# Attention: high and low halves of the turned weights side by side in one tile, one matmul of 512 columns for both

## The reference, cut to what matters

```
s = q[:, q0:q1] @ k[:, :q1].T                      # per head
s = s + cum[q0:q1, None] - cum[None, :q1]          # forget gate sums
p = softmax(where(causal, s, -inf))
o[q0:q1] = p @ v[:, :q1]
return (o * silu(gate)) @ w_out
```

## Time and profile before

| | us |
|---|---|
| median of 3 runs | 2338.66 (2337.63 to 2339.77) |
| the profiled execution | 2337.15 |
| its span | 2335.4 |
| PE busy in the span | 2318.9 (99%) |
| DVE, ACT, POOL busy | 1349.1 (58%), 1114.3 (48%), 621.9 (27%) |
| the attention, first V to last | about 748 to 1525 |

### The profile page before, as it was taken

The page is one execution under the profiler, slowest core; times in us unless marked ns, Lnnn a source line. Parts: engine busy times, 40 slices in busy tenths (PEclk is TensorE's granted clock), DMA queues, the critical chain, the costliest instruction groups (busy, mean ns, idle before and its releaser), DMA issues. The chain is left out here.

```text
span 2335.4 us, 36441 instructions
## 1 busy us (share of the span) xinstructions
PE 2318.9 (99%) x13373; PEld 2026.8 (87%) x13373; DVE 1349.1 (58%) x2772; ACT 1114.3 (48%) x2060; POOL 621.9 (27%) x718
## 2 busy tenths in 40 slices
PE   9999999999999999999999999999999999999998
PEld 7888889999887999999999999988888888888887
DVE  4221121232012999899998999956535565768733
ACT  2111111231113989889898898822024565657300
POOL 0000000010000455566556665536410000000344
PEclk9999999999999999999999999999999999999999
DMA  6444443242216365456654566286624354448672
GB/s 209 138 130 111 118 126 113 105 136 104 68 64 168 90 143 122 116 128 149 144 120 117 128 147 147 87 257 198 209 81 136 114 156 133 135 136 307 211 235 98
DMA packets 221306, 328.77 MB, mean 141 GB/s; under 512 B 17469, under 2 KB 144765, under 8 KB 215309
## 3 DMA queue, kind: packets, MB, share of 16 engines
q1 hardware_dynamic: 220616, 325.91, 48.7%
q0 software_dynamic: 512, 0.53, 0.1%
HBM read 199.89 MB, written 126.48 MB: 140 GB/s over the span
## 5 line engine op out<-in xcount | busy, mean ns | idle before, releaser
L1018 DVE TENSOR_TENSOR at_pl<-at_tps,at_ph 128x512 fp32r<-128x512 f32 (+3 forms) x640 | 372.0, 602 | 27.5 <-ACT at_ph L919 27.4
L919 ACT ACTIVATE at_ph<-at_tps 128x512 fp32r<-128x512 f32 (+3 forms) x640 | 317.3, 534 | 63.1 <-PE at_ops L849 41.7
L380 ACT ACTIVATE pa_stg<-pa_ps 128x512 fp32r<-128x512 f32 (+1 forms) x120 | 71.7, 598 | 575.4 <-PE pa_ps L272 569.5
L829 PE MATMUL at_tps<-ident,at_probs 128*128 128x128 f32 x2176 | 328.5, 273 | 1.3 <-ACT at_probs L909 1.3
L849 PE MATMUL at_ops<-at_ph,at_val 128*128 128x256 f32 (+1 forms) x1152 | 322.9, 298 | 1.4 <-DVE at_pl L1018 1.4
L909 ACT ACTIVATE at_probs<-at_probs,at_least 128x128 f32<-128x128 f32 (+15 forms) x256 | 308.4, 1205 | 17.5 <-DVE at_least L1007 17.5
L849 PE MATMUL at_ops<-at_pl,at_val 128*128 128x256 f32 (+1 forms) x1152 | 299.7, 281 | 0.0
L272 PE MATMUL pa_ps<-pa_xh,pa_wh 128*128 128x512 f32 x760 | 298.8, 393 | 0.0
L272 PE MATMUL pa_ps<-pa_xh,pa_wl 128*128 128x512 f32 x760 | 297.3, 391 | 0.0
L272 PE MATMUL pa_ps<-pa_xl,pa_wh 128*128 128x512 f32 x760 | 296.9, 391 | 0.0
L829 PEld LDWEIGHTS at_tps<-ident,at_probs 128*128 128x128 f32 x2176 | 256.1, 140 | 25.1 <-ACT at_probs L909 1.6
(11 more groups left out here) (203 smaller groups left out, 4553.1 us busy)
## 6 DMA issues: line engine op xcount, KB each, us to landing
at_q<-q_halves SPq DMA_DIRECT2D x45, 512.0 KB
at_k<-k_halves SPq DMA_DIRECT2D x45, 512.0 KB
q_halves<-pa_stg SPq DMA_DIRECT2D x32, 512.0 KB, 3.8
k_halves<-pa_stg SPq DMA_DIRECT2D x32, 512.0 KB, 3.7
v_halves<-pa_stg SPq DMA_DIRECT2D x32, 512.0 KB, 2.9
y_gated<-re_work SPq DMA_DIRECT2D x32, 512.0 KB, 2.9
at_val<-v_halves SPq DMA_DIRECT2D x15, 1024.0 KB, 13.3
pa_wst<-in_attn_w_in SPq DMA_DIRECT2D x14, 1024.0 KB, 7.1
```

Of the source, the lines that this page charges most:

```text
L380: nc.scalar.activation(out, source(kind, s), func, scale=scale).then_inc(evac_h, 1)
L829: mm = nc.tensor.transpose(tps[c % TB][:, k, :], probs[s % ROWS][:, t0:t0 + P], ident[:, :])
L919: nc.scalar.activation(ph[g % 2][:, j * PB:j * PB + n, i % 2 * P:(i % 2 + 1) * P], tps[c % TB][:, 0:n, :], ACT.Copy).then_inc(high_out, 1)
L1018: nc.vector.tensor_tensor(pl[g % 2][at], tps[c % TB][:, 0:n, :], raw(ph[g % 2][at]), ALU.subtract)\
```

## The change

- `ph` and `pl` become one tile `halves[b]` of 128 x 2 x 16 x 256, with the high half at index 0 and the low half at 1. H and L write the same shapes as before, into it.
- Each key tile has one matmul with the 2 x 256 columns of both halves, into the whole bank `ops[b]`: columns 0 to 255 are the sum over the high halves, 256 to 511 the sum over the low ones. In the last key tile it is 2 x 128 columns.
- M's first copy takes 64 x 2 x 256 instead of 64 x 256; its second part goes to one of two extra slots of `att`. M's second copy is as before, and takes the columns of the high half alone: the product of low values and low weights, which was in the sum before, is left out.
- POOL adds the two parts of `att` with one more addition, and waits for it before it adds `low_sum`.
- The transposed inverse sums of group n (n % 4 == 2) go to the other bank, `ops[1 - b]`, since `ops[b]` is full. So PE waits for the move of group n - 1 before the transpose, and before the first V of group n + 1, which writes `ops[1 - b]`, it waits for the copy of the inverse sums. The wait before the groups with n % 4 == 0 goes.
- The tiles in SBUF are put in another order; the unused space shrinks from 5 x 128 to 128 elements.

```diff
@@ weigh (PE)
-                    if g % HG == 0:
-                        wait(pe, rden_out, (it * GROUPS + g) // HG)
+                    if g % HG == HG - 1:
+                        wait(pe, rden_out, (it * GROUPS + g) // HG + 1)
                 for kt in range(lo, hi):
                     c0 = P if kt == KT - 1 else 0
-                    for t in (ph, pl):
-                        mm = nc.tensor.matmul(ops[b][:, 0, c0:GW], val[hp][:, kt, :], t[b][:, kt, c0:GW],
-                                              start=(kt == 0 and t is ph), stop=(kt == KT - 1 and t is pl))
+                    mm = nc.tensor.matmul(ops[b][:, :, c0:GW], val[hp][:, kt, :], halves[b][:, :, kt, c0:GW],
+                                          start=(kt == 0), stop=(kt == KT - 1))
                 if hi == KT:
                     mm.then_inc(weighed, 1)
                     if g % HG == HG - 2:
                         f = (it * GROUPS + g) // HG
                         wait(pe, rden_ready, f + 1)
-                        nc.tensor.transpose(ops[b][0:2 * HG, 1, 0:P], rden[:, f % 2, :], ident[:, :]).then_inc(rden_turned, 1)
+                        wait(pe, moved, 2 * (it * GROUPS + g))
+                        nc.tensor.transpose(ops[1 - b][0:2 * HG, 0, 0:P], rden[:, f % 2, :], ident[:, :]).then_inc(rden_turned, 1)
@@ move (ACT)
-                    nc.scalar.activation(rden_rows[:, f % 2, :], ops[b][0:2 * HG, 1, 0:P], ACT.Copy).then_inc(rden_out, 1)
+                    nc.scalar.activation(rden_rows[:, f % 2, :], ops[1 - b][0:2 * HG, 0, 0:P], ACT.Copy).then_inc(rden_out, 1)
                 wait(act, summed, n - 1)
                 wait(act, gated, 2 * (n - AR + 1))
-                nc.scalar.activation(att[:, n % AR, :], ops[b][0:HEAD_DIM, 0, :], ACT.Copy).then_inc(moved, 1)
+                slot, extra = n % AR, AR + n % 2
+                nc.scalar.activation(att[:, slot:extra + 1:extra - slot, :], ops[b][0:HEAD_DIM, :, :], ACT.Copy)\
+                    .then_inc(moved, 1)
@@ add_halves (POOL)
                 pool.wait_ge(moved, 2 * n + 2)
+                nc.gpsimd.tensor_tensor(att[:, n % AR, :], att[:, n % AR, :], att[:, AR + n % 2, :], ALU.add)\
+                    .then_inc(joined, 1)
+                pool.wait_ge(joined, n + 1)
                 nc.gpsimd.tensor_tensor(att[:, n % AR, :], att[:, n % AR, :], low_sum[:, n % 2, :], ALU.add)\
                     .then_inc(summed, 1)
```

More of the change, by code:

```diff
@@ L572, in attend @@
         a = Alloc(nc, ctx, stage)
-        q1, q2, k1, k2, val, probs, ph, pl = ({} for _ in range(8))
+        q1, q2, k1, k2, val, probs, halves = ({} for _ in range(7))
         def rows(t, name, k, dt=F32R):
@@ L579, in values, with turned_rows @@
             val[k] = a.sb(f"val{k}", [P, QT, P], F32R)
-        def turned_rows(t, name, k):
-            t[k] = a.sb(f"{name}{k}", [P, QT, GW], F32R)
+        def turned_rows(k):
+            halves[k] = a.sb(f"turned{k}", [P, 2, QT, GW], F32R)
         rows(q1, "q1_", 0)
@@ L589, in attend @@
         rows(k2, "k2_", 1)
-        turned_rows(ph, "ph", 0)
+        values(1)
+        rows(probs, "probs", 1, F32)
         rows(q1, "q1_", 1)
         rows(q2, "q2_", 1)
-        turned_rows(pl, "pl", 0)
-        values(1)
-        rows(probs, "probs", 1, F32)
+        turned_rows(0)
         rows(k2, "k2_", 0)
         values(0)
-        turned_rows(ph, "ph", 1)
-        turned_rows(pl, "pl", 1)
+        turned_rows(1)
         for k in range(2, ROWS):
@@ L604, in attend @@
         scale = a.sb("scale", [HEAD_DIM, 2, HG, GW])
-        att = a.sb("att", [HEAD_DIM, AR, GW])
+        att = a.sb("att", [HEAD_DIM, AR + 2, GW])
         y = a.sb("y", [HEAD_DIM, GW])
@@ L609, in attend @@
         rden_rows = a.sb("rden_rows", [2 * HG, 2, P])
-        a.sb("free", [P, 5 * P])
+        a.sb("free", [P, P])
         mask = a.sb("mask", [P, BANK])
@@ L647, in attend @@
         moved = a.sem("moved")
+        joined = a.sem("joined")
         summed = a.sem("summed")
@@ L918, in high @@
                 wait(act, turned, it * CH + c + 1)
-                nc.scalar.activation(ph[g % 2][:, j * PB:j * PB + n, i % 2 * P:(i % 2 + 1) * P],
+                nc.scalar.activation(halves[g % 2][:, 0, j * PB:j * PB + n, i % 2 * P:(i % 2 + 1) * P],
                                      tps[c % TB][:, 0:n, :], ACT.Copy).then_inc(high_out, 1)
@@ L1016, in low @@
                 wait(dve, high_out, it * CH + c + 1)
-                at = (slice(None), slice(j * PB, j * PB + n), slice(i % 2 * P, (i % 2 + 1) * P))
-                nc.vector.tensor_tensor(pl[g % 2][at], tps[c % TB][:, 0:n, :], raw(ph[g % 2][at]), ALU.subtract)\
+                high_, low_ = (halves[g % 2][:, l, j * PB:j * PB + n, i % 2 * P:(i % 2 + 1) * P] for l in range(2))
+                nc.vector.tensor_tensor(low_, tps[c % TB][:, 0:n, :], raw(high_), ALU.subtract)\
                     .then_inc(low_out, 1)
```

## The result

| | us |
|---|---|
| before, median of 5 runs | 2337.63 (2336.47 to 2339.77) |
| after, median of 5 runs | 2394.18 (2388.93 to 2396.90) |
| ratio | 1.0235, 95% interval 1.0223 to 1.0247 |
| the profiled execution, its span | 2389.48, 2387.7 (before 2337.15, 2335.4) |

Forecast was 2381, range 2366 to 2400, so the median is 13 us above the forecast and inside the range. The profiled execution took 52.3 us more than that of before.

What follows compares the result with a forecast made beforehand. The prediction took PE to set the attention's pace, DVE and ACT close behind. 2337.15 + 45.8 (Place A) + 6.4 (Place B) + 1.4 (end) - 11.3 (PE's stream) = 2379.5, plus 1.5 for the median: 2381 us, range 2366 to 2400.

Steps and rivals of the forecast that it cites:

- Place A: Groups n % 8 == 2: next group's first V waits for ACT's inverse-sums copy, 2.86 us, 16 times, 45.8 us.
- Place B: Groups n % 8 == 6: the same wait ahead of the next group's first V, 0.40 us, 16 times, 6.4 us.
- PE's stream: PE's own instructions get 11.3 us shorter: 4.1 us from full key tiles, 7.2 us from last key tiles of groups.
- POOL's second addition: One more 730 ns addition per group: nothing inside the attention, 1.4 us at its end.
- the prediction's estimate of 3 us for two additions: At the attention's end, contention with DVE over SBUF could make POOL's two additions take 3 us instead of 1.5.
- DVE and ACT should hold PE up no more than they do now: Inside the attention: after each stop DVE and ACT trail PE by less than before, so no added cost.
- The forecast's rival of a fast kernel: ACT runs ahead and its inverse-sums copy is in time at Place A: 2328 to 2334 us, 6%.
- The rival that made ACT the pace: ACT's 1.7 us of extra copying is added in each head: +27 us, about 2408 us, 5%.
- The clock: Rival: half speed after each of 16 stops, 1.5 to 2.9 us each, +23 to +47 us, 2404 to 2428, 6%.
- the clock stays at 1.00 throughout: Sign expected in PE's timeline after the change: the granted clock remains at 1.00.

Runs made afterwards that it cites:

- e2_wait: Kernel before, with only PE's wait for the copy of the inverse sums moved ahead of the next group's first V: 2388.38 us, ratio 1.0213.
- e3_narrow: Changed kernel, but ACT's first copy takes only the high half and POOL adds `low_sum` twice: 2379.52 us, ratio 1.0179.
- e7_free_pairs: e6_free with two matmuls of 256 columns in place of one of 512: 2346.87 us, ratio 1.0037.
- e6_free: Changed kernel, inverse sums transposed into a narrow chunk's free `tps` quarter, each head's second transpose moved into the next head, the last unchanged: 2337.58 us, ratio 0.9999.
- e10_free_narrow: e6_free, but ACT's first copy takes only the high half and POOL adds `low_sum` twice: 2331.76 us, ratio 0.9976.
- e12_end: e11_onecopy, but DVE makes the sums of the last two groups in place of POOL: 2330.33 us, ratio 0.9969.
- e1_tps: Changed kernel, inverse sums transposed into a narrow chunk's free `tps` quarter, both within the same head, without PE's waits for bank and copy: 2353.96 us, ratio 1.0067.
- e11_onecopy: e6_free with the last inverse-sums load issued ahead of group 122's store, one whole-bank ACT copy per group, three POOL additions: 2335.93 us, ratio 0.9992.
- e5_early: Changed kernel with ACT's copy of the inverse sums taken ahead of the exponential: 2347.94 us, ratio 1.0042.

## Why the forecast was right, and what it missed

- Place A: forecast a stop of 2.86 us in each of 16 heads, measured 2.78. Its parts: the lateness that the trace of before held already (2.23) is confirmed by e2_wait, whose stop is 2.4; for the wider copy e3_narrow shows 0.33 us at the stop and 0.44 in the head where 0.43 was forecast; the latency was put at 0.06 from a release by DVE, and is 0.15 from the end of ACT's copy (916.61) to the V (916.76).
- Place B: forecast 0.40, measured 0.42.
- PE's stream: forecast 0.70 us less per head (11.3 / 16); e7_free_pairs against e6_free shows 0.61. Inside the changed kernel the head is 51.27 where the forecast was 51.3.
- POOL's second addition: nothing inside, 1.4 us at the end forecast, 1.55 measured. Of the four additions of the last two groups one met DVE's subtraction and took 1.60 us (1573.14), the others 0.73; so the prediction's estimate of 3 us for two additions, by the contention, did not come true here.
- "DVE and ACT should hold PE up no more than they do now": true in the changed kernel (48.73 + 2.78 + 0.42 - 0.61 = 51.32 explains its head of 51.27), and false without its stops. That the stops are what gives ACT the time is concluded from this contrast. The forecast's rival of a fast kernel, 2328 to 2334, took the whole 11 us as kept. e6_free, e7_free_pairs and e10_free_narrow show that ACT's wider copy eats 0.4 of the 0.6 us. The rival that made ACT the pace put that copy at 1.7 us per head, four times as much.
- The clock: the rival was priced as a fall after each of 16 stops, at 1.5 to 2.9 us, and given 6%. It came true in part: 7 falls at 1.6 us in the profiled execution and, as an estimate from the 7.4 us between them, some five more in the slowest. This is the 10 us by which the profiled execution exceeds its forecast of 2379.5, and most of the 13 us of the median. The sum itself had no term for it, and its sign "the clock stays at 1.00 throughout" did not hold. That the median still lies in the range is partly luck: the range had that room for longer stops and a smaller gain, not for the clock. What the prediction had wrong here is to have taken "falls" and "falls not" as the only cases. The rows read then, 1.22 us of idle time without a fall and over 4 us with one, left 2.8 us in between.

Falls are not bound to stops of that length either. In e12_end PE's clock fell at the start of the attention, behind idle times of which the longest is 1.25 us; the kernel before has the same idle times there and kept 2.4 GHz (the second line):

```profile
742.50:745.50 3.00, 3.00 (x11) 2.39 (x11) 1.56 (x6) 1.56 (x5) 0.11 (x1) 0.50 0.84 209
741.00:750.00 9.00, 7.24 (x41) 5.52 (x42) 6.75 (x21) 6.11 (x17) 1.67 (x1) 1.00 0.84 191
```

The same fall is in the profiled executions of e1_tps, e6_free, e7_free_pairs and e11_onecopy, the last with the lower level from 743 to 752. A difference of a few us between two single executions can be such falls alone; the medians above rest on 4 to 21 runs.

What stays open: that a fall follows six of 16 like stops is observed, but not what picks them. To fill the stops with other PE work, which would show whether the idle time itself brings the falls, wasn't tried.

## What to carry to other kernels

Before a matmul is widened to a whole PSUM bank, ask what else lived in that bank: here a transpose of 8 rows, moved next door, made PE wait ahead of every fourth group for a small copy that stood late in another engine's hand-made list, and cost five times what the wider matmul saves. A wait is priced by the order of the engine that ends it; that lateness could be read to 0.1 us from two timelines of the kernel before. And when three engines are all nine tenths busy or more, an edit that spares the first and loads the second is worth only what the second can take.

## What the runs showed of the hardware

- Stops of 2.4 to 2.8 us, from start to start, brought PE to 1.2 GHz near the end of some of them and not of others: four of 16 in e3_narrow, five in e2_wait, six in the changed kernel. A fall cost 1.6 us where a head with one was set beside a head without. With stops of 0.9 us (e5_early) it did not happen in the attention. At the attention's start it came in five of the 13 profiled executions, with idle times of at most 1.25 us.
- ACT's copy of 64x512 out of PSUM takes 582 ns (the changed kernel), one of 128x512 takes 599 ns (e11_onecopy): twice the rows cost 17 ns, so one copy of all 128 rows does what two copies of 582 and 382 ns did.
- POOL's additions of 64x256 take 0.73 us, and 1.60 us beside DVE's subtraction of two SBUF inputs (1573.14 above). The Trainium skill (GPSIMD Engine Reference, 8. Key points) states that contention; these rows agree.
